# The opening of a two-layer trunk in another order, and weight rests made by VectorE alone

## What is computed

```python
mod_l = silu(c) @ w_ada[layer] + b_ada[layer]        # and mod_c from c_ctx
sh1, sc1, g1, sh2, sc2, g2 = split(mod_l, 6)
h = modulate(rms_norm(x, norm1[layer]), sh1, sc1)    # latent and context rows
p = split_columns(h @ w_in[layer])                   # mLSTM q,k,v,o,gates; attention q,k,v; conv u,B,C; three gates
y_m, y_a, y_c = mlstm(p), attention(p), short_conv(p)
x = x + g1 * ((sum_b sigmoid(gate_b) * (y_b @ w_proj_b)) @ w_out[layer])
x = x + g2 * (square(relu(modulate(rms_norm(x, norm2), sh2, sc2) @ w_up)) @ w_down)
# the context rows take the same path in layer 0; at the end rms_norm(x, final_norm)
```

## Time and profile before

| | us |
|---|---|
| median of 3 runs | 1948.4 (1947.9 to 1950.41) |
| the profiled execution | 1943.74 |
| its span, first to last instruction | 1941.9 |
| TensorE busy | 1872.9 |
| mean granted clock of TensorE, share of full | 0.986 |

### The profile page before, as it was taken

How to read it: one execution, slowest core, us unless ns; L and a number is a source line. 1 busy time by engine, 2 the same in 40 slices (tenths; PEclk the granted TensorE clock), 3 DMA queues, 4 the chain that set the end, 5 groups by cost and what they waited for, 6 DMA issues and landing times.

```text
span 1941.9 us, 27168 instructions
## 1 busy us (share of the span) xinstructions
PE 1872.9 (96%) x11175; PEld 1607.7 (83%) x11175; DVE 979.1 (50%) x1372; ACT 689.9 (36%) x946; POOL 729.6 (38%) x513
## 2 busy tenths in 40 slices
PE   5999899999999999999999999999999999979998
PEld 3697688778878788778877778799997999969997
DVE  4454543645433443366443544644657656547554
ACT  3333532433222232243232222433543444434443
POOL 2332231112543344544222322432332566746553
PEclk7999999999999999999999999999999999989999
DMA  9221122122444334465225337222232355565562
GB/s 315 66 88 44 44 66 73 58 65 66 150 132 130 111 127 147 135 197 169 91 90 184 107 118 240 81 94 88 66 122 97 109 181 189 174 195 173 177 191 91
DMA packets 240858, 244.64 MB, mean 126 GB/s; under 512 B 6020, under 2 KB 239840, under 8 KB 240736
## 3 DMA queue, kind: packets, MB, share of 16 engines
q1 hardware_dynamic: 240432, 242.80, 39.5%
q10 hardware_dynamic: 304, 0.10, 0.0%
HBM read 241.83 MB, written 1.05 MB: 125 GB/s over the span
## 4 chain that ended last, share of the span: by engine, by line
PE 89%; DVE 4%; SPq 2%; issue 1%; ACT 1%; DMA 1%; POOL 1%; DVEq 0%; ACTq 0%; POOLq 0%
PE pp L931 19%; PE pp L935 19%; PE pp L932 19%; PE pp L939 4%; PE pp L938 4%; PE pp L940 4%; PE pc L1099 3%; PE pp L913 2%; PE pp L915 2%; PE pp L914 2%; SPq L827 2%; PE pc L1020 2%; PE pc L1151 1%; PE pc L1189 1%; DVE wL L1605 1%
## 5 line engine op out<-in xcount | busy, mean ns | idle before, releaser
L1492 POOL TENSOR_TENSOR wL<-raw,wH 128x512 fp32r<-128x512 f32 x360 | 580.2, 1632 | 854.4 <-ACT wH L1203 854.3
L931 PE MATMUL pp<-hH,wH 128*128 128x512 f32 (+1 forms) x1760 | 590.5, 346 | 19.3 <-ACT hH L1388 14.3
L1605 DVE TENSOR_TENSOR wL<-raw,wH 128x512 fp32r<-128x512 f32 x360 | 459.2, 1299 | 266.4 <-ACT wH L1203 261.0
L932 PE MATMUL pp<-hH,wL 128*128 128x512 f32 (+1 forms) x1760 | 582.1, 341 | 0.0
L1203 ACT ACTIVATE wH<-raw 128x1024 fp32r<-128x1024 f32 x360 | 360.3, 1049 | 336.0 <-PE pp L940 222.1
L935 PE MATMUL pp<-hL,wH 128*128 128x512 f32 (+1 forms) x1760 | 457.2, 341 | 2.6 <-POOL hL L1543 1.7
L931 PEld LDWEIGHTS pp<-hH,wH 128*128 128x128 f32 x1760 | 335.6, 191 | 66.8 <-issue 17.8
L932 PEld LDWEIGHTS pp<-hH,wL 128*128 128x128 f32 x1760 | 336.0, 191 | 37.1 <-issue 1.0
L935 PEld LDWEIGHTS pp<-hL,wH 128*128 128x128 f32 x1760 | 304.7, 191 | 44.2 <-POOL hL L1543 6.6
L938 PE MATMUL pp<-yH,wH 128*128 128x512 f32 (+1 forms) x448 | 150.6, 336 | 0.0
L939 PE MATMUL pp<-yL,wH 128*128 128x512 f32 (+1 forms) x448 | 150.6, 336 | 0.0
(11 more groups left out here) (228 smaller groups left out, 2097.3 us busy)
## 6 DMA issues: line engine op xcount, KB each, us to landing
raw<-in_w_in SPq DMA_DIRECT2D x84, 1024.0 KB, 5.2
raw<-in_w_up SPq DMA_DIRECT2D x32, 1024.0 KB, 5.6
raw<-in_w_down SPq DMA_DIRECT2D x32, 1024.0 KB, 5.2
ada_T<-in_w_ada SPq DMA_DIRECT2D x18, 1024.0 KB, 7.9
ada_G<-in_w_ada SPq DMA_DIRECT2D x12, 1024.0 KB, 8.5
ada_Y<-in_w_ada SPq DMA_DIRECT2D x10, 1024.0 KB, 13.0
ada_H<-in_w_ada SPq DMA_DIRECT2D x8, 1024.0 KB, 9.2
raw<-in_w_proj_m SPq DMA_DIRECT2D x8, 1024.0 KB, 5.2
```

Source lines behind the costliest of these rows:

```text
L931: pe.matmul(dsts[b], wh[b], hi[:, kt, ts_], start=first, stop=False)
L932: pe.matmul(dsts[b], wl[b], hi[:, kt, ts_], start=False, stop=False)
L1492: pool.tensor_tensor(wL[:, p % RAW, ks, :], raw[:, p % RAW, ks, :], wH[:, p % HIGH, ks, :].bitcast(F32), ALU.subtract).then_inc(wL_ready, 1)
L1605: dve.tensor_tensor(wL[:, p % RAW, ks, :], raw[:, p % RAW, ks, :], wH[:, p % HIGH, ks, :].bitcast(F32), ALU.subtract).then_inc(wLv_ready, 1)
```

## The change

The head's list is put in another order. The third `w_ada` piece is multiplied behind `mean`, and the fourth behind `spread`. Three warm-up multiplications (identity by x_in, into a PSUM bank that nobody reads) follow the first turn. The second `w_ada` half (four pieces and its turn) moves from behind both `head` steps to between them. SyncE loads the second half of w_ada ahead of panel 1. The rests of panel 0 are made by GpSimd alone, all later rests, in both layers, by VectorE alone, in pieces of 128x1024. The split of the gate weights is a step of its own, behind all of `apply`. VectorE waits in the first rotary step for the last y of the mLSTM branch, which its wait for GpSimd's rests had implied.

```diff
@@ make_plan, layer 0
-            ada(3)
+            ada(2)
             step("mean", l, n=1)
             ada()
+            step("spread", l, n=1)
+            ada()
             step("adarow", l, g=0)
-            step("spread", l, n=1)
             step("adaturn", l, g=0)
             step("modulation", l, g=0)
+            step("warm", l)
             step("first_split", l, p=0)
             step("apply", l, n=1, j=0)
             step("apply", l, n=1, j=1)
+            head("mk", l, 0)
+            ada(4)
             step("first_split", l, p=1)
-            heads(l, 1)
-            ada(4)
             ada_end(1)
+            head("mk", l, 1)
             step("apply", l, n=1, j=2)
             step("apply", l, n=1, j=3)
             step("first_rest", l)
         else:
             spread_apply(l, 1, 2)
+        step("gate_w", l)
         panel("mk", l, 0)
@@ SyncE
             load_panel(0)
-            load_panel(1)
             for a in range(NC, FIRST_ADA):
                 load_ada(a)
+            load_panel(1)
@@ TensorE
-                        pe.wait_ge(wL_ready, 2 * p + kt // KH + 1)
-                        pe.wait_ge(wLv_ready, 2 * p + kt // KH + 1)
+                        if p == 0:
+                            pe.wait_ge(wL0_ready, kt // KH + 1)
+                        else:
+                            pe.wait_ge(wL_ready, 2 * p - 1 + kt // KH)
...
+                elif k == "warm":
+                    for i in range(WARM):
+                        pe.matmul(pp[:, 1, 1, :], ident, x_in[:, 0, 0:TOK], start=True, stop=True)
@@ ScalarE (the three lines leave apply, n == 1, j == 0)
+                elif k == "gate_w":
+                    act.wait_ge(s_wg, 80 * (l + 1))
+                    act.wait_ge(wgz_ready, l + 1)
+                    act.activation(wg[:, :, 0:16], w_gate[:, :, :], ACT.Copy).then_inc(wgH_ready, 1)
@@ GpSimd
-            def split(st):
-
-                p = st["p"]
+            def first_rest():
+
                 for i in range(2):
-                    ks = slice(i * KH, i * KH + KP)
+                    ks = slice(i * KH, (i + 1) * KH)
...
                 if k == "panel":
-                    nx = next_panel(st)
-                    if nx:
-                        split(nx)
...
+                elif k == "gate_w":
+                    pool.wait_ge(wgH_ready, l + 1)
+                    pool.tensor_tensor(wg[:, :, 32:48], w_gate[:, :, :], wg[:, :, 0:16].bitcast(F32),
+                                       ALU.subtract).then_inc(wg_ready, 1)
@@ VectorE
-                    ks = slice(i * KH + KP, (i + 1) * KH)
+                    ks = slice(i * KH, (i + 1) * KH)
...
-                elif k == "first_split":
+                elif k == "first_split" and st["p"]:
                     split(PANELS[st["p"]])
...
+                    if qk_order.index(j) == 0:
+                        dve.wait_ge(y_ready, y_no[l, "m", MH - 1] + 1)
```

More of the change, by code:

```diff
@@ L49 @@
 KH = KT // 2
-KP = 2
+WARM = 3
 SIZES = dict(mq=512, mk=512, mv=1024, mo=1024, mg=16, aq=1024, ak=256, av=256, cu=D, cb=D, cc=D, g0=D, g1=D, g2=D)
@@ L205, in ada_end, with head @@
             step(k, 0, g=g)
+    def head(kind, l, c, b=0):
+        panel(kind, l, c, b, k="head")
     def heads(l, n):
-        for kind, c, b in ((("mk", 0, 0), ("mk", 1, 0)) if n == 1 else (("up", 0, 0), ("up", 1, 0))):
-            panel(kind, l, c, b, k="head")
+        for c in range(2):
+            head("mk" if n == 1 else "up", l, c)
     def spread_apply(l, n, fill=0):
@@ L607, in trunk @@
         ot_ready = sem("h_turned_scaled")
-        wLv_ready = sem("weights_rest_vector_ready")
+        wL0_ready = sem("first_weights_rest_ready")
         sq_ready = sem("squares_ready")
@@ L1390, in _ @@
                             i.then_inc(hc_ready if v == 0 and len(norm_halves(st)) == 2 else hH_ready, 1)
-                    if st["n"] == 1 and j == 0:
-                        act.wait_ge(s_wg, 80 * (l + 1))
-                        act.wait_ge(wgz_ready, l + 1)
-                        act.activation(wg[:, :, 0:16], w_gate[:, :, :], ACT.Copy).then_inc(wgH_ready, 1)
+                elif k == "gate_w":
+                    act.wait_ge(s_wg, 80 * (l + 1))
+                    act.wait_ge(wgz_ready, l + 1)
+                    act.activation(wg[:, :, 0:16], w_gate[:, :, :], ACT.Copy).then_inc(wgH_ready, 1)
                 elif k == "gate_exp":
@@ L1484, in _ @@
             pool.memset(eps, EPS).then_inc(s_const, 1)
-            def split(st):
-                p = st["p"]
+            def first_rest():
                 for i in range(2):
-                    ks = slice(i * KH, i * KH + KP)
-                    pool.wait_ge(wH_ready, 2 * p + i + 1)
-                    pool.tensor_tensor(wL[:, p % RAW, ks, :], raw[:, p % RAW, ks, :], wH[:, p % HIGH, ks, :].bitcast(F32),
-                                       ALU.subtract).then_inc(wL_ready, 1)
+                    ks = slice(i * KH, (i + 1) * KH)
+                    pool.wait_ge(wH_ready, i + 1)
+                    pool.tensor_tensor(wL[:, 0, ks, :], raw[:, 0, ks, :], wH[:, 0, ks, :].bitcast(F32),
+                                       ALU.subtract).then_inc(wL0_ready, 1)
             def y_rest(no, src, kts, ts_):
@@ L1523, in _ @@
                         y_rest(y_no[l, "c", c_], y_tmp[:, :, ts_], slice(2 * c_, 2 * c_ + 2), ts_)
-                elif k == "first_split":
-                    split(PANELS[st["p"]])
+                elif k == "first_split" and st["p"] == 0:
+                    first_rest()
                 elif k == "apply":
@@ L1544, in _ @@
                                            ALU.subtract).then_inc(h_ready, 1)
-                    if st["n"] == 1 and j == 0:
-                        pool.wait_ge(wgH_ready, l + 1)
-                        pool.tensor_tensor(wg[:, :, 32:48], w_gate[:, :, :], wg[:, :, 0:16].bitcast(F32),
-                                           ALU.subtract).then_inc(wg_ready, 1)
                     if st["n"] == 1 and j == NC - 1:
@@ L1602, in split @@
                 for i in range(2):
-                    ks = slice(i * KH + KP, (i + 1) * KH)
+                    ks = slice(i * KH, (i + 1) * KH)
                     dve.wait_ge(wH_ready, 2 * p + i + 1)
                     dve.tensor_tensor(wL[:, p % RAW, ks, :], raw[:, p % RAW, ks, :], wH[:, p % HIGH, ks, :].bitcast(F32),
-                                      ALU.subtract).then_inc(wLv_ready, 1)
+                                      ALU.subtract).then_inc(wL_ready, 1)
             n_norm = n_half = n_nt = 0
```

## The result

The changed kernel takes 1928.74 us (median of 4 executions, 1926.52 to 1929.68), the kernel before 1949.41 beside it: ratio 0.989, 95% interval 0.9875 to 0.9906. The forecast was 1932.7 with a range from 1929.4 to 1938.5.

The account below looks back on a forecast made before the run. TensorE, busy 96%, was taken as the bound, so only its idle and lower-clock time could be won. 12.4 + 1.8 + 0.9 + 0.6 = 15.7 us off 1943.74 gave 1928.0; plus 4.7 carried, 1932.7, range 1929.4 to 1938.5.

Parts of the forecast that it names:

- The head (12.4): Start of the kernel up to the first gate product: the new order brings that product from 75.30 to 62.9, winning 12.4 us.
- Step 2: Head, warm-ups: three multiplications start at 30.4, end at 35.3 at half clock, and bring full clock for what follows.
- step 3: Head, first half of panel 0: done at 40.8, both by TensorE's work from 35.3 and by the operands from 31.5.
- 31.5 and not 33.6: Head, first n_t: 31.5 if GpSimd's rests hold VectorE until 31.2; 33.6 at the latest if the memset behind holds it too.
- Output projection of layer 1 (1.8): Layer 1, output projection: the merged add no longer waits for GpSimd's rests, so it and all behind start 1.8 us earlier.
- Attention of layer 1 (0.9): Layer 1, attention: rests before the copy to prT take 2.45 for 3.44 us, cutting TensorE's 1.20 us wait by 0.9.
- Elsewhere (0.6): Other places: VectorE operations freed from being held by GpSimd's rests win 0.6 us together, between -1.5 and +2.
- single long rest ahead of something urgent: Outside the head and the two named layer 1 places: the low case of the 0.6 us estimate, a loss of 1.5 us.
- The sum (15.7): Whole kernel: 12.4 + 1.8 + 0.9 + 0.6 = 15.7 us off the profiled execution of 1943.74 us, giving 1928.0.
- I carry that difference: Whole kernel: the unprofiled median's 4.7 us above the profiled execution was added to 1928.0, giving 1932.7.
- my last sign: Forecast wrong if the clock drops to 0.5 after 40 us, first n_t passes 33.6, or TensorE newly waits for wL in layer 1.
- Only the head gains: Rival, chance 0.12: outside the head, VectorE's longer single instruction costs what the freed port gives, so 1936.0 us.

Follow-up runs that it names:

- No_warm: The changed kernel without its three warm-up multiplications: median 1927.2 us, ratio 0.9899 against the kernel before.
- head_only: The changed kernel with each panel's rests shared between VectorE and GpSimd as before: median 1935.5 us, ratio 0.993 against the kernel before.
- vector_rests: The kernel before with only the rests moved to VectorE alone (panel 0's to GpSimd): median 1940.47 us, ratio 0.9958 against the kernel before.
- before_warm: The kernel before with eight warm-up multiplications added in its two waits of half panel 0: median 1947.83 us, ratio 0.9996 against the kernel before.
- before_look3: A further profiled execution of the kernel before, with no edit: 1942.48 us.

## Why the prediction was right and wrong, by its own steps

**The head (12.4): right, 12.85 measured.** First n_t 31.18 (31.5 said): GpSimd's rests held the gain to 31.0 as foreseen (its two operations took 1.09 us at 30.05 and 0.24 at 46.30, where GpSimd was at rest). Half panel 0 done at 40.76 (40.8), the w_ada half at 44.42 (44.5), VectorE free at 45.0 (45.0), turn done at 46.0 (46.1), gate product 62.45 (62.9; the 0.4 for handoffs did not come). Step 2 was wrong: the clock had risen at 27 and the warm-ups ended at 32.4, not 35.3. It cost nothing, since the second path of step 3, by the operands, gave 40.8 too, and that is the one that held; that the two paths met in one figure was luck. No_warm shows that the warm-ups are idle cargo.

On the Trainium skill's rule ("SBUF — State Buffer", "Who interferes with whom": whoever issues first holds the ports, the other blocks): n_t came at 31.18, so 31.5 and not 33.6 was the side to take. The same section says that a GpSimd instruction that only writes doesn't contend, which I had not used. n_t is no test of it, since its second operand (pc) lies in PSUM; the second gain operation is one, and the trace agrees: with both operands in SBUF it began at 30.99, beside the memset, and took 0.15 us, as it does at 46.4 (0.16). But a row of the kernel before does not fit so easily:
```profile
69.58 6.59 DVE L1605 TENSOR_TENSOR wL<-raw,wH 128x512 fp32r<-128x512 f32 x1
```
This rest began beside memsets, a microsecond ahead of GpSimd's own rests at 70.59, and outlasted all four of them, where alone it takes 0.69 us. Why it was not done before 70.59 stays open. In the trace the rule also worked against the change, at a place I had not seen (below).

**Output projection of layer 1 (1.8): right.** From gs to the transfers it was 1703.68 - 1698.53 = 5.15 us and is now 1691.67 - 1688.21 = 3.46; the waits behind went from 6.91 to 6.30 and from 4.31 to 2.94.
```profile
1687.53 0.68 DVE L1677 SCALAR_TENSOR_TENSOR gs<-gs,pp 128x512 f32<-128x512 f32 x1
```
```profile
1691.67 0.99 SPq L835 DMA_DIRECT2D ada_G<-in_w_ada  x2
```

**Attention of layer 1 (0.9): too small.** The wait of 1.20 is gone, as said. A second one, 2.07 in all but the executions where a drop hides it, is now 0.97. That is 2.3 us. It is 2.3 between the two profiled executions as well, though before had the drop: from the first of these products to the fourth it took 35.42 us (1445.49 to 1480.91), now 33.15 (1436.58 to 1469.73). The row at 1457.73 in the profile of before showed products of twice their length, and I did not ask what stood behind them.
```profile
1447.71 1.96 PE L1164 MATMUL pc<-k_a,q_a 128*128 128x512 f32 x4
...
1458.99 1.96 PE L1164 MATMUL pc<-k_a,q_a 128*128 128x512 f32 x4 [0.97 <-DVE prT L2015]
```

**Elsewhere (0.6): about right as a net.** Won: a wait of 0.61 for hH at 1702, 0.5 ahead of the last turn, 0.35 ahead of the last column sums. Lost: a new stop of 1.12 us in layer 1.
```profile
1326.05 2.99 POOL L1575 TENSOR_SCALAR_AFFINE_SELECT EP<-EP 128x128 f32<-128x128 f32 x4 [85.70 <-DVEq L1909]
1326.07 2.58 DVE L1614 TENSOR_TENSOR wL<-raw,wH 128x1024 fp32r<-128x1024 f32 x2 [0.23 <-DVE EP L1901]
...
1329.15 6.30 PE L1112 MATMUL pc<-vaug,EP 128*128 128x257 f32 x28 [1.12 <-issue]
```
GpSimd's four selects take 2.99 us beside VectorE's long rests, and TensorE's product needs what they make. In head_only, beside rests of half the length, they take 1.93, and there is no such stop, while vector_rests has it. It is the "single long rest ahead of something urgent" of my lower bound, only with GpSimd as the one that is held.

**The sum (15.7) against 13.9.** The terms for work were not too high; the attention's was too low. Two drops of the clock took more in the profile after: 10 x 0.32 = 3.2 us from 130 to 140 and as much from 1300 to 1310, where before had 1.7 and 1.8. They more than cover the 1.8 us.
```profile
130.00:140.00 10.00, 10.00 (x61) 9.98 (x61) 2.65 (x3) 0.00 (x0) 0.00 (x0) 0.68 0.10 34
...
1300.00:1310.00 10.00, 10.00 (x62) 9.84 (x61) 3.88 (x4) 2.00 (x2) 0.00 (x0) 0.68 0.35 107
```

**The failing step: "I carry that difference".** 4.7 us was no constant between a profiled execution and the median. Single executions of before scatter over 9 us (1942.5 to 1951.9), its profiled ones lay low again and again, and none of that carried over: after the change the difference is -0.9. By itself it makes 5.6 us of error; the profile that was 1.7 us longer than forecast takes some back, and 4.0 remain. The range allowed 1.5 us for this scatter, where the executions shown for before already stood 4.2 us and more above the profiled one. That the head (forecast 12.4, head_only 13.6) was nearly right and the rests (forecast 3.3, vector_rests 8.2) were not is the same miss seen between medians; how much of the 8.2 is the scatter of before stays open.

**The rivals and signs.** None decided. In the head the clock did not fall after 27 us. Further on it did fall to 0.5, which my last sign called wrong without saying where: at 130 and 1300 us, as in before at much the same places. No wait of TensorE for wL turned up in layer 1. "Only the head gains" is refuted by vector_rests. Panel 1's landing does sit on the chain, but at 41.5 as reckoned. VectorE did not become the bound: it is 49% busy.

## What to carry to other kernels

Don't add the gap between one profiled execution and a median to a forecast: put it into the range, with the scatter of single executions, and look at where in the profile the clock drops fell and whether a wait swallowed them. Look first for a wait for something nobody needs yet: here the gate weights were about half of the whole gain (9.4 us alone), against some 4 for the interleaving and nothing measurable for the warm-ups. In these runs keeping the clock up bought nothing ahead of an operand that comes late (no_warm, before_warm), while a drop under a TensorE with no wait behind it cost its full length.

## What was not expected of the hardware

- The granted clock drops under a TensorE that is 100% busy, at much the same places of the program in each execution (130 to 150, 1300 to 1330 us) but not in all, each time at a loss of 1.7 or some 3.3 us; before_look3 and vector_rests had none from 1300 to 1330. What sets them off is not shown.
- Eight warm-ups raised the mean clock by 0.003 and the time stayed the same.
- The hold between VectorE and GpSimd works both ways: four GpSimd selects took 2.99 us beside two VectorE subtractions of 128x1024, and 1.93 beside two of 128x512.
